# Block attention in a two-block layer kernel on one core: queries held backwards, the bias added by VectorE, 64-row products on alternate halves, the last softmax round ahead of its slabs, value slabs 512 columns wide

## The chip, the cores and the metric

One core of one Trainium2 chip runs the whole kernel. The metric is the device time of one execution in microseconds (us); lower is better. The profiled execution is one more execution, whose trace is read below.

## What is computed

Two transformer-like blocks on 256 tokens of width 1024. The change touches the first half of the first block, `hybrid_layer`, and there above all the block attention:

```
h = rmsnorm(x, norm_mix)
proj = h @ w_in                       # 27 slabs of 256 columns
qa, ka, va, ra, a_lr, qb, kb, vb, gates = split(proj)
oa = gla_chunked(qa, ka, va, log_a)   # 4 heads, chunks of 64 tokens, kv products k^T v
# block attention: 8 heads of 64, one block of 256 keys, so all keys are "own"
logit = qb @ kb^T * 64 ** -0.5 + bias_tab[:, t5_bucket(q_pos - k_pos)]
logit = where(k_pos <= q_pos, logit, -1e30)
ob = softmax(logit) @ vb
mixed = sigmoid(g_a) * (oa @ w_branch_gla) + sigmoid(g_b) * (ob @ w_branch_moba)
```

After it come w_out, two gated conv feed-forwards, a conformer block and a window attention of the second model. None of their code is changed.

## The kernel before, in words

All weights come from memory as slabs of 1 MB (128 partitions x 2048 floats) in a ring of three buffers (`raw`). A slab of the "mix" kind is split for precision: ScalarE copies it to `whi` (L785), VectorE and GpSimd subtract one half each into `wlo` (L1205, L743), and TensorE then makes three products for each 128x128 piece (`mm3`, L1776 to L1778: hi by hi, hi by lo, lo by hi). A slab of the "ada" kind is used unsplit, by TensorE's L1910. The order is written out by hand: every engine runs down the same list `LEAD` of 51 items, in which mix slabs g0 to g26 alternate with ada slabs until ada 23 stands between g21 and g22; g23 to g26 follow each other directly. An engine that waits in one item holds all that stands behind it in its own queue. ScalarE and VectorE split the slab three places ahead (`hi(Slab(n + RING))`, `lo(Slab(n + RING))`) at the start of each item.

Between the slabs, small pieces of the two attentions are hung on numbers g:

- g5 to g8 are the value slabs of the first attention and g13, g14 those of the block attention. `tokens` keeps the tokens still and streams 256 columns, 48 products a slab, into half a PSUM bank for each of the two token tiles; ScalarE copies each slab out (`drain`, L929). Items with a mix slab use banks 0 and 2 in turn, and a slab waits until the mix slab two before it was copied out (`mix_drained`).
- g10 and g11: the state products of the first attention (L2009), 64 rows of k each, first the four heads of chunk 0 (rows 0 to 63), then those of chunk 1 (rows 64 to 127), then at g11 chunk 2.
- g15, g18 and g21: the scores of the block attention in three rounds. Round 0 has queries 0 to 127 of 8 heads against 128 keys, rounds 1 and 2 have queries 128 to 255 of 4 heads each against 256 keys. For each head two f32 products go into the same place in PSUM banks 4 and 5: the 64-row product of query and key (L2064, even heads in rows 0 to 63 and bank 4, odd heads in rows 64 to 127 and bank 5), and a 128-row product of a reversing matrix `rev` with `brev`, the bias rows by distance, which adds the bias (L2066).
- `less_max` on VectorE: row maximum (L1445) and scores less maximum into `state` (L1449). ScalarE makes exponentials of it (L996). VectorE then sums, inverts and multiplies (L1528, L1530, L1532) and releases `p_done`. TensorE turns the result in eight transposes (L2048) into banks 6 and 7, and ScalarE copies these out (L1002). `less_max` of rounds 0, 1, 2 stands at g16, g19, g22, the normalising at g17, g20, g23, the transposes at g18, g21, g24, and the product with the values at g25 (L2078).

## Time and profile before

| | us |
|---|---|
| median of 3 runs | 1451.29 |
| the runs | 1450.57 to 1452.48 |
| the profiled execution | 1450.95 |
| its span, first to last instruction | 1449.2 |
| TensorE matmuls busy | 1398.1 (96%) |
| VectorE, ScalarE, GpSimd busy | 981.4, 824.7, 575.6 |
| mean granted TensorE clock | 0.991 of 2.4 GHz |

Busy time is time in which at least one instruction of the engine was under way. Consecutive matmuls overlap, so for their cost the distance of their starts counts, not the duration of one. The granted clock is either 1.00 or half; a mean between tells how much of the stretch was at half.

### The profile page before, as it was taken

How to read it: one execution, taken by the hardware profiler on the slowest of the kernel's cores; microseconds unless marked ns; L12 is line 12 of the kernel's file. 1: busy time of each engine (PE TensorE's matmuls, PEld its weight loads, DVE VectorE, ACT ScalarE, POOL GpSimd, SP SyncE). 2: the span in 40 equal slices, each digit the busy share in tenths (PEclk: the TensorE clock that was granted, in tenths of full speed). 3: DMA queues.
4: the chain of work that ended last, by engine and by line, in shares of the span. 5: the costliest groups of instructions: out<-in, count | busy, mean ns of one | idle time of the engine just before them, and what ended most of it. 6: DMA issues, size and time to landing. Idle time of an engine off the chain costs nothing.

```text
span 1449.2 us, 27974 instructions
## 1 busy us (share of the span) xinstructions
PE 1398.1 (96%) x11062; PEld 1310.0 (90%) x11062; DVE 981.4 (68%) x1302; ACT 824.7 (57%) x1179; POOL 575.6 (40%) x192
## 2 busy tenths in 40 slices
PE   5999999999999999999999999999999898999997
PEld 3899888999999999999999998999997757899997
DVE  3312554666889987859899977665665684765665
ACT  4632354555778856567888465545544474555543
POOL 2443334365422222453222233655654201465562
PEclk9999999999999999999999999999999999999999
DMA  7784565345344445674444455655545401544550
GB/s 283 270 313 185 222 234 204 146 176 187 123 172 171 173 175 200 252 275 162 170 166 169 162 204 219 233 203 208 224 177 223 186 30 59 198 181 175 188 187 30
DMA packets 39144, 272.09 MB, mean 188 GB/s; under 512 B 4436, under 2 KB 5588, under 8 KB 6414
## 3 DMA queue, kind: packets, MB, share of 16 engines
q1 hardware_dynamic: 39054, 270.81, 49.8%
q8 instruction: 66, 1.08, 0.3%
q14 instruction: 24, 0.20, 0.0%
HBM read 269.73 MB, written 1.06 MB: 187 GB/s over the span
## 4 chain that ended last, share of the span: by engine, by line
PE 86%; DVE 5%; ACT 4%; DMA 2%; POOL 1%; issue 1%; SPq 0%; DVEq 0%; ACTq 0%
PE ps L1776 22%; PE ps L1777 22%; PE ps L1778 22%; PE ps L616 9%; PE ps L1910 3%; ACT whi L785 2%; POOL wlo L743 1%; DMA raw<-w_dram 1%; PE ps L1813 1%; PE ps L2244 1%; DVE wlo L1205 1%; PE ps L2232 1%; DMA mv<-b_forget_dram 1%; PE ps L2066 1%; PE ps L2064 1%
## 5 line engine op out<-in xcount | busy, mean ns | idle before, releaser
L743 POOL TENSOR_TENSOR wlo<-raw,whi 128x1024 fp32r<-128x1024 f32 (+1 forms) x183 | 573.4, 3136 | 849.2 <-ACT whi L785 849.1
L785 ACT ACTIVATE whi<-raw 128x2048 fp32r<-128x2048 f32 x183 | 349.3, 1910 | 415.2 <-PE ps L1778 233.5
L1205 DVE TENSOR_TENSOR wlo<-raw,whi 128x1024 fp32r<-128x1024 f32 (+1 forms) x183 | 288.0, 1574 | 325.0 <-ACT whi L785 324.4
L1776 PE MATMUL ps<-h_hi,whi 128*128 128x256 f32 x1248 | 360.2, 289 | 4.8 <-POOL wlo L743 4.8
L1777 PE MATMUL ps<-h_lo,whi 128*128 128x256 f32 x1248 | 354.6, 284 | 0.0
L1778 PE MATMUL ps<-h_hi,wlo 128*128 128x256 f32 x1248 | 354.3, 284 | 0.0
L1776 PE MATMUL ps<-g_hi,whi 128*128 128x256 f32 x1040 | 298.4, 287 | 5.8 <-POOL wlo L743 2.6
L1777 PE MATMUL ps<-g_lo,whi 128*128 128x256 f32 x1040 | 294.9, 284 | 0.0
L1778 PE MATMUL ps<-g_hi,wlo 128*128 128x256 f32 x1040 | 294.8, 283 | 0.0
L1776 PEld LDWEIGHTS ps<-h_hi,whi 128*128 128x128 f32 x1248 | 240.9, 193 | 13.3 <-issue 12.8
L1777 PEld LDWEIGHTS ps<-h_lo,whi 128*128 128x128 f32 x1248 | 241.0, 193 | 0.5
L1778 PEld LDWEIGHTS ps<-h_hi,wlo 128*128 128x128 f32 x1248 | 240.9, 193 | 0.0
L1776 PEld LDWEIGHTS ps<-g_hi,whi 128*128 128x128 f32 x1040 | 200.1, 192 | 10.1 <-issue 6.9
L1777 PEld LDWEIGHTS ps<-g_lo,whi 128*128 128x128 f32 x1040 | 200.2, 192 | 0.3
L1778 PEld LDWEIGHTS ps<-g_hi,wlo 128*128 128x128 f32 x1040 | 200.2, 192 | 0.0
L616 PE MATMUL ps<-cvb,raw 128*128 128x256 f32 x704 | 155.3, 379 | 0.0
L616 PEld LDWEIGHTS ps<-cvb,raw 128*128 128x128 f32 x704 | 132.5, 190 | 17.3
L1776 PE MATMUL ps<-m_hi,whi 128*128 128x256 f32 x384 | 108.7, 283 | 0.0
L1777 PE MATMUL ps<-m_lo,whi 128*128 128x256 f32 x384 | 108.7, 283 | 0.0
L1778 PE MATMUL ps<-m_hi,wlo 128*128 128x256 f32 x384 | 108.7, 283 | 0.0
L533 DVE SCALAR_TENSOR_TENSOR cvb<-ps,cols,cvb 128x255 f32<-128x255 f32 (+1 forms) x176 | 76.5, 476 | 11.3 <-ACT cvb L455 6.7
L879 ACT ACTIVATE bufB<-gates,cols 128x256 f32 (+1 forms) x176 | 72.7, 499 | 17.9 <-DVE sra L1327 17.9
(270 smaller groups left out, 1958.7 us busy)
## 6 DMA issues: line engine op xcount, KB each, us to landing
raw<-w_dram SPq DMA_DIRECT2D x247, 1024.0 KB, 4.8
brev<-w_dram SPq DMA_DIRECT2D x2, 1024.0 KB, 6.8
gates<-w_dram SPq DMA_DIRECT2D x2, 1024.0 KB, 7.7
xlat<-xT_dram SPq DMA_DIRECT2D x1, 1024.0 KB, 4.9
brev<-bias_rows SPq DMA_DIRECT2D x1, 1024.0 KB, 8.9
brev<-ctxT_dram SPq DMA_DIRECT2D x1, 1024.0 KB, 10.2
sra<-w_dram SPq DMA_DIRECT2D x1, 1024.0 KB, 7.2
mqk<-w_dram SPq DMA_DIRECT2D x1, 1024.0 KB, 6.7
```

Source lines behind the costliest of these rows:

```text
L533: ins = dve.scalar_tensor_tensor(out, ps[:, 2 * par + half, m * T + src:m * T + src + n], w, out, ALU.mult, ALU.add)
L616: ins = pe.matmul(ps[:, 4 + m // 2, (m % 2) * T:(m % 2) * T + T], wf[:, k, m * P:m * P + P], cvb[:, par, k, :], start=(first and k == 0 an ...
L743: pool.tensor_tensor(wlo[:, g.slot, part], raw[:, g.slot, part], whi[:, g.slot, part].bitcast(F32), ALU.subtract).then_inc(lo2_done, 1)
L785: act.activation(whi[:, g.slot, :], raw[:, g.slot, :], ACT.Copy).then_inc(hi_done, 1)
L879: ins = act.activation(buf[:, t * T:t * T + T], vpad[:, t, bass.ds(k, T)], ACT.Copy, scale=w)
L1205: dve.tensor_tensor(wlo[:, g.slot, part], raw[:, g.slot, part], whi[:, g.slot, part].bitcast(F32), ALU.subtract)\
L1776: pe.matmul(out, w[0], x[0], start=start, stop=False, skip_group_check=True)
L1777: pe.matmul(out, w[0], x[1], start=False, stop=False, skip_group_check=True)
L1778: return pe.matmul(out, w[1], x[0], start=False, stop=stop, skip_group_check=True)
L1813: pe.matmul(ps[:, bank, m * T:m * T + T], w[i][:, k, m * P:m * P + P], x[0][:, k, :], start=(k == 0 and m == 0 and i == 0), stop=False, sk ...
L1910: ins = pe.matmul(ps[r:r + QUAD, bank, 0:SLABC], cnd[:, c:c + QUAD], w[:, t, :], start=(t < 4 and k == 0), stop=(t >= 4 and k == n - 1), s ...
L2064: pe.matmul(out, mqk[r0:r0 + DH, 0, h // 2, q0:q0 + P], mqk[r0:r0 + DH, 1, h // 2, 0:nk], start=(i % 512 == 0), stop=False, skip_group_che ...
```

## The change

Five edits, all in the stretch up to about 250 us.

1. The queries of the block attention are stored with each 128-token half reversed (`backwards`, a negative step in ScalarE's output). The scores then have the row order that the bias rows in `brev` already have, and `rev` and the products L2066 are gone. After the scores, VectorE adds `brev` to the scores in PSUM (a 128x1024 addition ahead of the row maximum in `less_max`); the wait for the bias rows moves from TensorE to VectorE. ScalarE's copy of the transposed probabilities writes backwards, so what follows is as it was.
2. The score products, now all of 64 rows, alternate between rows 0 to 63 and 64 to 127 from head to head. The state products at g10 do so too: for each head chunk 0, then chunk 1.
3. Round 2's `less_max` and normalising both move to the item ada 23 (from g22 and g23), ahead of VectorE's split of that item; its exponentials move there too on ScalarE. The transposes and their copy move from g24 to g23.
4. The value slabs hold 512 columns by half of the input width, two to a group. `tokens_wide` streams 512 columns, 24 products a slab, into banks 0 and 2. Both are copied out after the second slab of the pair (`drain_wide`), and the first slab of a pair waits for `mix_drained` once more before its second token tile.
5. The load of `xctx` into the buffer of `brev` waits for the last `less_max`, not for the last scores.

```diff
+        def backwards(a):
+            *outer, (step, n) = a.ap
+            return bass.AP(a.tensor, a.offset + step * (n - 1), [*outer, [-step, n]])
...
-                    sp.wait_ge(sc_done, 3)
+                    sp.wait_ge(sub_done, 3)
...
+            def drain_wide(out):
+                for s in range(2):
+                    act.activation(out[:, s, :], ps[:, 2 * s, :], ACT.Copy).then_inc(mix_drained, 1)
...
+                if (kind, g) == ("ada", N_ADA - 1):
+                    exponentials(2)
                 hi(Slab(n + RING))
...
+                    turned_back = backwards(flat(pt_of(r)).rearrange("p (a x) -> p a x", x=P))
+                    act.activation(turned_back, flat(ps[:, 6:8, :]).rearrange("p (a x) -> p a x", x=P), ACT.Copy).then_inc(pt_sb, 1)
...
+                dve.wait_ge(brev_in, 16)
                 dve.wait_ge(sc_done, r + 1)
+                order.mark(dve.tensor_tensor(by_parity, by_parity, bias, ALU.add))
+                dve.wait_ge(dve_order, order.value())
                 order.mark(dve.tensor_reduce(tiny[:, 32:32 + nb], sc, AX.X, ALU.max))
...
+            def tokens_wide(g, i, x, second):
+                w = weights(g, 4)
+                for s in range(2):
+                    if s and not i:
+                        pe.wait_ge(*second)
+                    for k in range(4):
+                        t = 4 * i + k
+                        ins = mm3(ps[:, 2 * s, :], [a[:, t, s * P:s * P + P] for a in x], [a[:, k, :] for a in w],
+                                  start=(t == 0), stop=(t == KT - 1))
+                ins.then_inc(slab_done, 1)
...
-                        tokens(Slab(AT[kind, g]), n % 4, H)
+                        tokens_wide(Slab(AT[kind, g]), 1 - g % 2, H, (mix_drained, g))
...
-                    for c in (0, 1) if g == 10 else (2,):
-                        s, r0 = c // 2, (c % 2) * CHUNK
-                        for h in range(H_GLA):
+                    for h in range(H_GLA):
+                        for c in (0, 1) if g == 10 else (2,):
+                            s, r0 = c // 2, (c % 2) * CHUNK
...
-                        pe.matmul(out, mqk[r0:r0 + DH, 0, h // 2, q0:q0 + P], mqk[r0:r0 + DH, 1, h // 2, 0:nk],
-                                  start=(i % 512 == 0), stop=False, skip_group_check=True)
-                        ins = pe.matmul(out, rev, brev[:, h, T - nk:T], start=False, stop=True, skip_group_check=True)
+                        ins = pe.matmul(out, mqk[r0:r0 + DH, 0, h // 2, q0:q0 + P], mqk[r0:r0 + DH, 1, h // 2, 0:nk],
+                                        start=(i % 512 == 0), stop=True, skip_group_check=True)
```

How the instructions stand on TensorE around round 1 of the scores (after slab g18), before; L2048 are the transposes of round 0, L1910 is the ada slab that follows:

```order
L2048 MATMUL ps<-consts,state 128x128 [waits probs_done]
L2048 MATMUL ps<-consts,state 128x128 x7
L2064 MATMUL ps<-mqk 128x256 [waits scores_less_max]
L2066 MATMUL ps<-brev,consts 128x256
L2064 MATMUL ps<-mqk 128x256
```

and after (the transposes are now L2089, the scores L2104, the ada slab L1951):

```order
L2089 MATMUL ps<-consts,state 128x128 [waits probs_done]
L2089 MATMUL ps<-consts,state 128x128 x7
L2104 MATMUL ps<-mqk 128x256 [waits scores_less_max]
L2104 MATMUL ps<-mqk 128x256 x3
L1951 MATMUL ps<-raw,cnd 32x256 [waits slab_landed1]
```

Where a score and a bias product alternated four times, four score products now stand together.

VectorE from the last `less_max` of round 1 to the end of round 2, before (L1205 is the split of a slab):

```order
L1445 TENSOR_REDUCE tiny<-ps 128x4 [waits scores_done]
L1449 TENSOR_TENSOR state<-ps,tiny 128x1024 [waits probsT_done,dve_order]
L1205 TENSOR_TENSOR wlo<-raw,whi 128x1024 [waits slab_hi_done]
L1528 TENSOR_REDUCE tiny<-state 128x4 [waits exp_done]
L1530 RECIPROCAL tiny<-tiny 128x4 [waits dve_order]
L1532 TENSOR_TENSOR state<-state,tiny 128x1024 [waits dve_order]
L1205 TENSOR_TENSOR wlo<-raw,whi 128x1024 [waits slab_hi_done] x2
L1445 TENSOR_REDUCE tiny<-ps 128x4 [waits scores_done]
L1449 TENSOR_TENSOR state<-ps,tiny 128x1024 [waits probsT_done,dve_order]
L1205 TENSOR_TENSOR wlo<-raw,whi 128x1024 [waits slab_hi_done]
```

and after, from the split of the slab ahead of round 2 (L1224 the split, L1468 the bias addition, L1482 to L1486 the normalising):

```order
L1224 TENSOR_TENSOR wlo<-raw,whi 128x1024 [waits slab_hi_done]
L1468 TENSOR_TENSOR ps<-ps,brev 128x1024 [waits scores_done,bias_landed]
L1470 TENSOR_REDUCE tiny<-ps 128x4 [waits dve_order]
L1474 TENSOR_TENSOR state<-ps,tiny 128x1024 [waits probsT_done,dve_order]
L1482 TENSOR_REDUCE tiny<-state 128x4 [waits exp_done]
L1484 RECIPROCAL tiny<-tiny 128x4 [waits dve_order]
L1486 TENSOR_TENSOR state<-state,tiny 128x1024 [waits dve_order]
L1224 TENSOR_TENSOR wlo<-raw,whi 128x1024 [waits slab_hi_done] x2
```

Round 2 goes one slab split earlier, in one piece, and each round begins with the addition.

ScalarE at the value slabs g5 to g8, before (L785 the split, L929 the copy out):

```order
L785 ACTIVATE whi<-raw 128x2048 [waits slab_used,slab_landed0]
L929 ACTIVATE gates<-ps 128x2x256 [waits slab_used]
L785 ACTIVATE whi<-raw 128x2048 [waits slab_used,slab_landed2]
L929 ACTIVATE gates<-ps 128x2x256 [waits slab_used]
L785 ACTIVATE whi<-raw 128x2048 [waits slab_used,slab_landed1]
L929 ACTIVATE gates<-ps 128x2x256 [waits slab_used]
```

and after (L790, L938):

```order
L790 ACTIVATE whi<-raw 128x2048 [waits slab_used,slab_landed0]
L790 ACTIVATE whi<-raw 128x2048 [waits slab_used,slab_landed2]
L938 ACTIVATE gates<-ps 128x512 [waits slab_used]
L938 ACTIVATE gates<-ps 128x512
L790 ACTIVATE whi<-raw 128x2048 [waits slab_used,slab_landed1]
```

The copies of a pair now stand together, behind the split that follows the pair's second slab in the list.

## Rows read from the trace of the kernel before

**Rows 1.** The page, busy time, share of the span, instructions, by engine.
```profile
PE 1398.1 (96%) x11062; PEld 1310.0 (90%) x11062; DVE 981.4 (68%) x1302; ACT 824.7 (57%) x1179; POOL 575.6 (40%) x192
```

**Rows 2.** Timeline, TensorE, round 0: start, duration, engine, line, operation, operands, count.
```profile
158.63 0.48 PE L2064 MATMUL ps<-mqk 64*128 64x128 f32 x2
...
165.30 1.07 PE L1910 MATMUL ps<-raw,cnd 128*32 128x256 f32 x16
```

**Rows 3.** Timeline, TensorE, round 1; then the 256-wide group of L2066, both rounds.
```profile
187.38 0.70 PE L2064 MATMUL ps<-mqk 64*128 64x256 f32 x2
...
192.40 1.07 PE L1910 MATMUL ps<-raw,cnd 128*32 128x256 f32 x16
...
L2066 PE MATMUL ps<-brev,consts 128*128 128x256 f32 x16 | 5.6, 431 | 0.0
```

**Rows 4.** Timeline, TensorE, the state products at g10 and at g11.
```profile
106.78 2.96 PE L2009 MATMUL ps<-gates,bufB 64*128 64x256 f32 x16
...
116.62 1.99 PE L2009 MATMUL ps<-gates,bufB 64*128 64x256 f32 x8
```

**Rows 5.** Timeline, TensorE, 64-row scores of the window attention, halves alternating.
```profile
1168.26 0.49 PE L2185 MATMUL ps<-m_hi,g_hi 64*128 64x512 f32 x2 [0.55 <-ACT tiny L1129]
1168.57 0.42 PE L2185 MATMUL ps<-m_lo,g_hi 64*128 64x512 f32 x2
1168.80 0.42 PE L2185 MATMUL ps<-m_hi,g_lo 64*128 64x512 f32 x2
```

**Rows 6.** Timeline, TensorE, 128-wide f32 products of one form.
```profile
125.38 0.60 PE L2022 MATMUL ps<-bufA,gates 128*128 128x128 f32 x4
```

**Rows 7.** Timeline, TensorE, value slab g7; then a group of two-pass f32 products.
```profile
77.23 0.28 PE L1777 MATMUL ps<-wlo,h_hi 128*128 128x256 f32 x1
77.35 0.28 PE L1778 MATMUL ps<-whi,h_lo 128*128 128x256 f32 x1
...
L616 PE MATMUL ps<-cvb,raw 128*128 128x256 f32 x96 | 21.2, 379 | 0.0
```

**Rows 8.** Timeline, ScalarE, while slab g6 is used.
```profile
75.07 1.91 ACT L785 ACTIVATE whi<-raw 128x2048 fp32r<-128x2048 f32 x1 [3.28 <-DMA raw<-w_dram]
76.88 0.58 ACT L929 ACTIVATE gates<-ps 128x512 f32<-128x512 f32 x1
```

**Rows 9.** Timeline, TensorE, round 2; window: length, busy by engine, clock, DMA.
```profile
241.36 1.89 PE L2048 MATMUL ps<-consts,state 128*128 128x128 f32 x8 [3.05 <-DVE state L1532]
242.90 0.56 PE L1776 MATMUL ps<-h_hi,whi 128*128 128x256 f32 x1
...
249.70 0.43 PE L2078 MATMUL ps<-state,mv 128*64 128x128 f32 x2
...
241.30:245.00 3.70, 3.64 (x18) 3.64 (x19) 3.31 (x2) 1.03 (x1) 2.22 (x1) 0.54 0.39 166
```

**Rows 10.** Timeline, TensorE, transposes of round 1.
```profile
213.01 0.28 PE L1778 MATMUL ps<-h_hi,wlo 128*128 128x256 f32 x1
213.31 1.09 PE L2048 MATMUL ps<-consts,state 128*128 128x128 f32 x8
```

**Rows 11.** Timeline, VectorE and ScalarE, round 1; the last is round 2.
```profile
206.86 1.21 DVE L1445 TENSOR_REDUCE tiny<-ps 128x4 f32<-128x1024 f32 x1
...
212.03 1.23 DVE L1532 TENSOR_TENSOR state<-state,tiny 128x1024 f32<-128x1024 f32 x1
...
209.36 1.06 ACT L996 ACTIVATE state<-state 128x1024 f32<-128x1024 f32 x1 [0.48 <-DVE state L1449]
...
226.46 3.71 ACT L785 ACTIVATE whi<-raw 128x2048 fp32r<-128x2048 f32 x2 [5.58 <-PE ps L1778]
```

**Rows 12.** One line's instructions, VectorE, PSUM and SBUF operands.
```profile
L1559 DVE TENSOR_TENSOR bufB<-ps,gates x2: 1210/1210/1211, 291.8 to 298.0; 128x1024 f32<-128x1024 f32 x2
```

**Rows 13.** Windows: length, busy PE PEld DVE ACT POOL, clock, DMA share, GB/s.
```profile
903.00:911.00 8.00, 6.16 (x41) 6.11 (x40) 7.28 (x6) 5.07 (x6) 7.62 (x3) 0.79 0.37 129
1202.00:1210.00 8.00, 6.54 (x57) 5.49 (x56) 3.89 (x12) 4.45 (x12) 0.00 (x0) 1.00 0.01 3
```

More of the change, by code:

```diff
@@ L324, in build @@
         wlr, alr = mv[0:RANK + 1, 0, :], mv[0:RANK + 1, 1, 0:T]
-        eye, rev, cum = (consts[:, i, :] for i in range(3))
+        eye, cum = (consts[:, i, :] for i in range(2))
         xctx = brev
@@ L1450, in less_max, with normalise @@
                    .then_inc(sub_done, 1)
+            def normalise(r):
+                nb = 8 if r == 0 else 4
+                pr = flat(state[:, 0, :, :]).rearrange("p (h k) -> p h k", h=nb)
+                dve.wait_ge(e_done, r + 1)
+                order.mark(dve.tensor_reduce(tiny[:, 40:40 + nb], pr, AX.X, ALU.add))
+                dve.wait_ge(dve_order, order.value())
+                order.mark(dve.reciprocal(tiny[:, 48:48 + nb], tiny[:, 40:40 + nb]))
+                dve.wait_ge(dve_order, order.value())
+                dve.tensor_tensor(pr, pr, tiny[:, 48:48 + nb, None].to_broadcast([P, nb, 1024 // nb]), ALU.mult)\
+                   .then_inc(p_done, 1)
             for n, (kind, g) in enumerate(LEAD):
[L1453 removed]
+                if (kind, g) == ("ada", N_ADA - 1):
                     less_max(2)
+                    normalise(2)
                 lo(Slab(n + RING))
@@ L2321 @@
                       (o_ra, V_W), (o_g, 2 * D)]:
+        if c0 in (o_va, o_vb):
+            for c in range(c0, c0 + width, 2 * SLABC):
+                for k in range(2):
+                    put("lead", AT["mix", i], win[k * D // 2:(k + 1) * D // 2, c:c + 2 * SLABC])
+                    i += 1
+            continue
         for c in range(c0, c0 + width, SLABC):
```

49 lines of the change are left out of this document (23 added, 26 removed).

## The prediction, made before the changed kernel ran

> **What bounds the kernel now.** I read the page first: TensorE is busy for 96% of the span, the next engine for 68% [rows 1]. So TensorE's own time counts nearly one for one, and work of the other engines counts only where TensorE waits for it. Then I went down TensorE's timeline at the places that the change touches, by distances of starts, since single durations overlap. Third I looked at the transposes, where TensorE meets the softmax: in round 2 it stands idle for 3.05 us until VectorE's multiplication ends, and the clock is at half for most of the 3.7 us behind that (mean 0.54, the 1.2 GHz level) [rows 9]. All the rest of the program is unchanged; I take its time as it is.
>
> **The change part by part**, against the profiled execution's span of 1449.2 us.
>
> *Score products.* Round 0 goes from 158.63 to 165.30: 6.67 us for 16 products, 0.417 each [rows 2]. Each f32 product is two records. Of one form, four 128-wide records stand in 0.60 us of which the last one's own length is about 0.28, so a record costs (0.60 - 0.28)/3 = 0.107 us [rows 6]; two would be 0.21. The other 0.2 us is what changing between 64 and 128 rows costs each time. Round 1 takes 192.40 - 187.38 = 5.02 us for 8 products, 0.627 each, and round 2 the same (x16 records of L2066 are two rounds) [rows 3]. Do products in different halves run at the same time? At g10 sixteen records, eight in each half one after the other, take 2.96 us; at g11 eight records of one half take 1.99. Two such groups in series would be nearly 4, so about 1.0 us already runs at the same time where the halves meet [rows 4]. And six 64x512 products in alternating halves start as three pairs, 0.31 and 0.23 apart, and are over 0.96 us after the first start [rows 5]; six in series at the 0.23 of one would need 1.4. So I count one half only. One 256-wide record more costs (1.99 - 0.70)/6 = 0.215 (eight records of one half less the first two [rows 3, 4]). Round 0: first product 0.417, six further records by 0.107, 1.06 us. Rounds 1 and 2: 0.627 + 2 x 0.215 = 1.06 each. Gain: 5.6 + 3.96 + 3.96 = **13.5 us**. If the halves did not overlap: round 0 0.417 + 14 x 0.107 = 1.9, the others 0.627 + 6 x 0.215 = 1.9, gain 11.0. If each change of half cost as a change of form does, half of the blocks goes: 8.4. I take 13.5, as rows 5 is the same pattern.
>
> *State products at g10.* Perfect alternation makes sixteen records as long as eight: 2.96 - 1.99 = **1.0 us** (between 0, if the queue already did what it can, and 1.0).
>
> *Value slabs.* Six slabs have 48 products of 256 columns, 0.12 us apart [rows 7]: 0.24 for two. A 512-wide one is not in the trace on full rows. From below: a two-pass f32 record, which also streams 512 column steps, costs 21.2/96 = 0.221 [rows 7]. From above: the last pair of half-array products came 0.23 after the one before [rows 5]. 144 products by 0.24 - 0.221 = 2.7 us, by 0.24 - 0.23 1.4. I take 0.221, the row on the full array: **2.6 us**. Off the path: ScalarE's copies, 1.16 where one 0.58 stood twice.
> TensorE: Matmul & The Clock Gate in the Trainium skill, section "Back-to-back issue gap", gives N/2.4 GHz plus about 2.5 ns, an estimate of 0.216 us for 512 columns; by it this term would be 3.5 us. The same rule makes 256 columns 0.109, where the trace has 0.12 [rows 7], so I don't take it; it is the page's form of the rival on cheaper products below.
>
> *The new wait behind a pair.* At g7 TensorE must have bank 0 back, which ScalarE now copies out only after g6. Before, the copy after g6 was at 76.88, held up by the split of a slab that landed at 75.07 (1.91 us), and ended at 77.46; g7's second product was at 77.23, so g7 began at about 77.0 [rows 7, 8]. That split is set by a landing, and the landing by an ada slab's end ahead of g6. g5 will be 0.44 us shorter, g6 too: the landing moves by the first, to 74.6, the copy ends at 77.0, and TensorE would be ready at 77.0 - 0.9 = 76.1. It waits **0.9 us** (0 to 1.1). Ahead of g9 and g15 stand the other products of g8 and g14, and they don't wait. Queued behind that wait are only TensorE's own slabs.
>
> *Round 2 ahead.* TensorE was idle for 3.05 us, counted from the last product's end; the next start could have been 0.28 - 0.12 = 0.16 ahead of that end (duration and distance in [rows 7]): 3.2 us. Behind that, at half clock, the transposes took 242.90 - 241.36 = 1.54 instead of about 1.0 (1.09 with the last one's tail in [rows 10]), and g25 249.70 - 242.90 = 6.80 instead of 48 x 0.12 + 0.2 = 5.9: 1.4 us. If the wait goes, so does the fall of the clock [rows 9]. What is late next? From the scores to the new place of the transposes TensorE has ada 23 (1.07 [rows 3]), g22 (5.9), two tiny products and g23 (5.9): 13 us. The chain needs the addition 1.22, maximum and difference 2.5, exponentials 1.1, sum to product 2.7 [rows 11, 12]: 7.6. It has 5 us to spare. What stands behind it: on ScalarE the split of g24, which waits for the end of g22 anyway (at 226.46) [rows 11], 6.9 us after the scores, and the exponentials end after 5. On VectorE its half of that split, due 8.9 us after the scores, when the chain has been through for 1.3 us; and g24 gets the transposes (1.0) as new cover. On SP the load of xctx goes out some 4 us later; behind it stand the loads of the first slabs after LEAD, which wait for the split of g24, later still. Gain: **4.6 us**.
>
> *The bias addition in rounds 0 and 1.* It costs 1.21 us as a PSUM and SBUF operation of the same size [rows 12], and with a short wait behind it 1.25. In round 0 ScalarE's exponentials wait for a slab's landing and split, several us after the difference is ready: hidden. In round 1 it is not: the transposes start at 213.31, just after VectorE's product ends (212.03 + 1.23), while the last slab product was at 213.01 and the next could have come at 213.13 [rows 10, 11]. The chain is already the later one by 0.18. The exponentials at 209.36 waited for the difference, so what is added there is added at its end. Against it, the slab whose landing starts the chain may come 0.3 us sooner, since the next load goes out later behind it. New wait 1.1 to 1.4 us, of which 0.18 was there: **-1.1 us**. Both ends of that lie below the idle time that was followed by half clock: 8.00 - 6.16 = 1.84 us idle and a mean clock of 0.79 in one stretch, 1.46 us idle and 1.00 in another [rows 13].
>
> *Writing backwards.* Five ScalarE copies of the same size; no row shows a negative step. At the old speed they cost nothing.
>
> **Sum:** 13.5 + 1.0 + 2.6 - 0.9 + 4.6 - 1.1 = 19.7 us. 1449.2 - 19.7 = 1429.5 of span; the profiled execution lies 1.75 over its span and the median 0.34 over that: 1431.6 us.
>
> **The rivals.**
> *Halves don't overlap for two-pass products, or not within one round.* For it: g10's overlap is only at the seam. Against: rows 5. Scores gain 11.0 and g10 nothing: 3.5 us less, 1435.1.
> *Round 1 becomes the new late chain and takes the clock along.* For it: 0.18 us of slack missing already, and the addition comes on top; if the landing is not sooner but 0.5 later, the wait is 1.9, and half clock for 3.4 us costs 1.5 more, as in round 2 [rows 9]: -2.2 us, 1433.8. Against: the idle of 1.46 that cost no clock [rows 13].
> *The wide slabs pay little:* 0.231 a product and both copies on the path: gain 1.4 - 1.1 instead of 1.7, 1433.0.
> *The wide products are still cheaper.* If column steps alone counted, 512 would cost what two of the 0.107 records of 256 steps cost [rows 6]: 0.214, a gain of 3.7 instead of 2.6, 1430.5. Against: the 0.221 of a 512-step record [rows 7].
> *Slower than before: ScalarE's reversed copies.* Place: the three copies of 1024 elements a partition, some 1.1 us each (0.58 for 512 [rows 8], 1.06 for exponentials of 1024 [rows 11]). The idle time behind them is of the order of the 5.58 us ahead of a split in rows 11. To eat up 19.7 us, each would have to take 5.5 + 19.7/3 = 12 us, eleven times as long. Nothing in the profile speaks for that; if it is twice as long it is hidden.
>
> **Chances.** My forecast 0.55; halves not overlapping 0.10; round 1 with clock 0.12; wide slabs poor 0.12; cheaper wide products or a fall of the clock fewer elsewhere 0.10; slower or no change 0.01. In the unchanged rest, waits like the 1.84 us one [rows 13] may keep or lose their fall of the clock, 1.5 us each. The range takes in these and the ends above: 1428.0 (cheap products, no wait at g7) to 1436.5 (halves in series and a poor round 1). A measurement can tell about 0.2%, 3 us, from no change; every case but the last is faster by more: faster 0.98, same 0.01, slower 0.01.
>
> **What would show it.** Right: no L2066; blocks of scores of 1.1 us; no wait of transposes in round 2, full clock there, and a wait of about 1.2 us in round 1; 0.9 us idle before g7; 512-wide products 0.22 apart. Wrong: blocks of 2 us (no overlap), half clock at round 1, a VectorE addition far over 1.2 us, ScalarE copies longer than 1.1 us that TensorE waits for.

## The result and the profile after

| | before | after |
|---|---|---|
| median | 1450.93 us (1450.04 to 1452.48, 4 runs) | 1431.95 us (1431.91 to 1432.49, 4 runs) |
| profiled execution | 1450.95 us, span 1449.2 | 1431.94 us, span 1430.2 |

The ratio is 0.9869, 95% interval 0.9855 to 0.9883: 19.0 us less, where the prediction said 19.7 (1431.6 us).

To see where the 19 us are, I cut each trace at two points of TensorE: the first product of slab g5 and the first product behind the attention (`ps<-mqk,ones`). The stretch between them holds the whole change.

| kernel | start of g5, us | stretch of the change, us | from there to the end, us |
|---|---|---|---|
| before | 63.13 | 207.81 | 1178.3 |
| after | 63.75 | 189.20 | 1177.3 |

18.6 us come from the stretch; the loads at the start took 0.6 more and the unchanged rest 1.0 less. In the fourteen traces of this case the start lies between 62.7 and 64.2 and the rest between 1176.2 and 1179.5, with no relation to what was changed. So the stretch, which is not touched by these, is what the comparisons below are made with, and a difference of under 2 us in medians says little.

The page after, TensorE's line (as rows 1):

```profile
PE 1379.1 (96%) x10886; PEld 1292.2 (90%) x10886; DVE 983.0 (69%) x1305; ACT 825.0 (58%) x1179; POOL 580.4 (41%) x192
```

TensorE's busy time fell by 19.0 us and its share stayed at 96%: it is still the bound.

**Score and state products.** Timeline of TensorE after, round 0, round 1 and g10 (start, duration, engine, line, operation, operands, count):

```profile
157.62 1.16 PE L2104 MATMUL ps<-mqk 64*128 64x128 f32 x16
158.71 0.42 PE L1951 MATMUL ps<-raw,cnd 128*32 128x256 f32 x4
...
180.76 1.13 PE L2104 MATMUL ps<-mqk 64*128 64x256 f32 x8
181.82 0.42 PE L1951 MATMUL ps<-raw,cnd 128*32 128x256 f32 x4
...
107.23 2.00 PE L2050 MATMUL ps<-gates,bufB 64*128 64x256 f32 x16
109.16 0.42 PE L1951 MATMUL ps<-raw,cnd 128*32 128x256 f32 x4
```

Against [rows 2] the block of round 0 is 158.71 - 157.62 = 1.09 us instead of 6.67, against [rows 3] rounds 1 and 2 are 1.06 instead of 5.02, and sixteen state records have the duration that eight had in [rows 4].

**Value slabs and the wait at g7.** Timeline of TensorE, then of ScalarE, after (as rows 7 and 8; L938 is `drain_wide`):

```profile
77.96 0.50 PE L1805 MATMUL ps<-whi,h_hi 128*128 128x512 f32 x1 [0.77 <-ACT gates L938]
78.30 0.40 PE L1806 MATMUL ps<-wlo,h_hi 128*128 128x512 f32 x1
78.53 0.40 PE L1807 MATMUL ps<-whi,h_lo 128*128 128x512 f32 x1
78.77 0.40 PE L1805 MATMUL ps<-whi,h_hi 128*128 128x512 f32 x1
...
75.52 1.91 ACT L790 ACTIVATE whi<-raw 128x2048 fp32r<-128x2048 f32 x1 [5.00 <-DMA raw<-w_dram]
77.33 1.07 ACT L938 ACTIVATE gates<-ps 128x512 f32<-128x512 f32 x2
```

The 512-wide products start 0.23 to 0.24 us apart. The six slabs together take 33.95 us instead of 35.46. Ahead of g7 TensorE waits 0.84 us (0.77 idle, the rest under the last product's tail).

**Round 1.** Timelines after of TensorE (L2089 are the transposes), VectorE, GpSimd and ScalarE (as rows 10 and 11; L1224 and L748 are VectorE's and GpSimd's half of the split of slab g22):

```profile
204.10 1.10 PE L2089 MATMUL ps<-consts,state 128*128 128x128 f32 x8 [1.38 <-DVE state L1486]
...
195.36 1.22 DVE L1468 TENSOR_TENSOR ps<-ps,brev 128x1024 f32<-128x1024 f32 x1
...
197.88 1.22 DVE L1474 TENSOR_TENSOR state<-ps,tiny 128x1024 f32<-128x1024 f32 x1
199.02 2.42 DVE L1224 TENSOR_TENSOR wlo<-raw,whi 128x1024 fp32r<-128x1024 f32 x1
201.36 1.21 DVE L1482 TENSOR_REDUCE tiny<-state 128x4 f32<-128x1024 f32 x1
...
197.95 2.40 POOL L748 TENSOR_TENSOR wlo<-raw,whi 128x1024 fp32r<-128x1024 f32 x1 [4.73 <-ACT whi L790]
...
195.96 1.91 ACT L790 ACTIVATE whi<-raw 128x2048 fp32r<-128x2048 f32 x1 [2.46 <-DMA raw<-w_dram]
```

The addition (L1468) takes 1.22 us. TensorE waits 1.54 us (1.38 idle and 0.16 under the tail), where it waited 0.18.

**Round 2** has no wait at all any more; the window has the clock at full speed, where rows 9 has 0.54 (window: length, busy PE PEld DVE ACT POOL, clock, DMA share, GB/s):

```profile
219.23 1.04 PE L2089 MATMUL ps<-consts,state 128*128 128x128 f32 x8
220.02 0.36 PE L1805 MATMUL ps<-h_hi,whi 128*128 128x256 f32 x1
...
218.00:222.00 4.00, 4.00 (x36) 4.00 (x35) 2.55 (x4) 3.43 (x5) 4.00 (x2) 1.00 0.49 162
```

**Writing backwards.** ScalarE's copy of the probabilities, by line after, the first of three (the others took 1018 and 1020 ns):

```profile
L1021 ACT ACTIVATE state<-ps x1: 1022/1022/1022, 185.0 to 185.0; 128x1024 f32<-128x1024 f32 x1
```

It took 1.02 us before too; the queries' copies take 0.578, like straight ones.

### The profile page after: what moved, and what is told of

Its sections match the earlier page's. It is cut to its first block, busy times and chain, and to the rows that moved or that the text cites. A ratio compares the mean times of both kernels' runs of the same rounds, so it can differ in the third digit from the quotient of the medians.

```text
span 1430.2 us, 27629 instructions
## 1 busy us (share of the span) xinstructions
PE 1379.1 (96%) x10886; PEld 1292.2 (90%) x10886; DVE 983.0 (69%) x1305; ACT 825.0 (58%) x1179; POOL 580.4 (41%) x192
## 3 DMA queue, kind: packets, MB, share of 16 engines
HBM read 269.66 MB, written 1.06 MB: 189 GB/s over the span
## 4 chain that ended last, share of the span: by engine, by line
PE 83%; ACT 5%; DVE 5%; DMA 3%; POOL 2%; issue 1%; DVEq 0%; SPq 0%; ACTq 0%
PE ps L1805 22%; PE ps L1806 21%; PE ps L1807 21%; PE ps L621 9%; DMA raw<-w_dram 3%; PE ps L1951 2%; ACT whi L790 2%; POOL wlo L748 2%; PE ps L1842 1%; PE ps L2283 1%; DVE wlo L1224 1%; PE ps L2271 1%; ACT bufA L1146 1%; PE ps L2224 1%; ACT mqk L871 1%
## 5 line engine op out<-in xcount | busy, mean ns | idle before, releaser
L748 POOL TENSOR_TENSOR wlo<-raw,whi 128x1024 fp32r<-128x1024 f32 (+1 forms) x183 | 578.2, 3163 | 825.4 <-ACT whi L790 825.2
L790 ACT ACTIVATE whi<-raw 128x2048 fp32r<-128x2048 f32 x183 | 349.5, 1911 | 413.3 <-PE ps L1807 226.0
L1224 DVE TENSOR_TENSOR wlo<-raw,whi 128x1024 fp32r<-128x1024 f32 (+1 forms) x183 | 280.7, 1535 | 308.1 <-ACT whi L790 306.5
L538 DVE SCALAR_TENSOR_TENSOR cva<-ps,cols,cva 128x255 f32<-128x255 f32 (+1 forms) x176 | 76.6, 477 | 9.0 <-ACT cva L460 4.3
```

The costliest lines, as they stand in the source:

```text
L538: ins = dve.scalar_tensor_tensor(out, ps[:, 2 * par + half, m * T + src:m * T + src + n], w, out, ALU.mult, ALU.add)
L748: pool.tensor_tensor(wlo[:, g.slot, part], raw[:, g.slot, part], whi[:, g.slot, part].bitcast(F32), ALU.subtract).then_inc(lo2_done, 1)
L790: act.activation(whi[:, g.slot, :], raw[:, g.slot, :], ACT.Copy).then_inc(hi_done, 1)
L1224: dve.tensor_tensor(wlo[:, g.slot, part], raw[:, g.slot, part], whi[:, g.slot, part].bitcast(F32), ALU.subtract)\
```

## The experiments

All ratios are to the kernel before, measured beside it. "Stretch" is the time from g5 to the end of the attention as above, 189.20 us in the changed kernel's first trace.

### 1. Were the form changes or the removed products the gain?

The kernel before, with the bias products behind all score products of a round:

```diff
                    for h in range(8) if r == 0 else range(4 * r - 4, 4 * r):
                        i = place(h, r) * nk
                        out = ps[:, 4 + i // 512, i % 512:i % 512 + nk]
...
                        pe.matmul(out, mqk[...], mqk[...], start=(i % 512 == 0), stop=False, skip_group_check=True)
+                   for h in range(8) if r == 0 else range(4 * r - 4, 4 * r):
+                       i = place(h, r) * nk
+                       out = ps[:, 4 + i // 512, i % 512:i % 512 + nk]
                        ins = pe.matmul(out, rev, brev[:, h, T - nk:T], start=False, stop=True, skip_group_check=True)
```

> The kernel before, with one edit: in each round the bias products stand behind all score products, not one behind each. The same products are made, so no work is saved; the form changes between 64 and 128 rows once a round instead of at each product, and score products of the two halves stand next to each other. Theory (the 0.2 us belongs to each change of form, and halves overlap): round 0 is 1.06 for the scores, 0.2 for the change, 16 records at 0.107, 3.0 us instead of 6.67; rounds 1 and 2 1.06 + 0.2 + 8 records at 0.215 = 3.0 instead of 5.02. Together 7.7 us less than before, of which round 2's part counts only if its softmax isn't late by as much: its transposes wait for a chain that starts with these scores, so that part, 2.0, may show as shorter idle time or not at all. 1443 to 1445. Rival (score products are dear in themselves, whatever stands between them): 5 to 6 us per round, the same time as before, 1451, and then the gain of the change came from the products that were left out.

Measured: 1441.97 us (1441.42 to 1442.26), ratio 0.9938 (0.9924 to 0.9951); stretch 200.22, 7.6 less than before. Timeline of TensorE in round 0:

```profile
159.37 1.16 PE L2064 MATMUL ps<-mqk 64*128 64x128 f32 x16
160.46 2.05 PE L2069 MATMUL ps<-brev,consts 128*128 128x128 f32 x16
```

The scores take 1.09 us, the bias products 1.98; rounds 1 and 2 take 2.98 instead of 5.02. That is 7.7 us less in the three blocks, as expected. The median is 9.0 less and lies under the 1443 to 1445 of the expectation; beside the stretch, the start took 0.7 more and the rest, which the edit doesn't touch, 2.0 less. So 7.6 of the 13.5 us were paid for switching between 64 and 128 rows and for the missing overlap, and could be had by reordering one loop, without VectorE's addition. The other 5.8 are the removed products themselves. How the 7.6 divide between the switching and the missing overlap, this run doesn't separate.

### 2. How far does the overlap of the halves reach?

The changed kernel with even heads, then odd heads, and g10 chunk by chunk:

```diff
-                    for h in range(H_GLA):
-                        for c in (0, 1) if g == 10 else (2,):
+                    for c in (0, 1) if g == 10 else (2,):
+                        for h in range(H_GLA):
...
-                    for h in range(8) if r == 0 else range(4 * r - 4, 4 * r):
+                    for h in sorted(range(8) if r == 0 else range(4 * r - 4, 4 * r), key=lambda h: h % 2):
```

> The changed kernel with the halves in groups: all even heads of a round, then all odd ones, and the state products at g10 chunk by chunk as before. Theory (products in different halves run side by side only where two groups meet): g10 0.97 longer as before. Score blocks: in series they would be 1.9 us each against 1.07 now, so at most 0.85 more each, 2.5 in all; with an overlap at the seam as at g10 of before (1.0 of 4.0), 0.5 us of each block is saved again, so about 0.4 each, 1.1 in all. Together UP by 1.0 + 1.1 to 2.5: 1434.0 to 1435.4. Rival (the score products were cheap because the form no longer changes, and alternation gives nothing): blocks stay 1.07, and only g10 moves.

Measured: 1432.78 us (1432.24 to 1435.39), ratio 0.988 (0.9865 to 0.9895). Timeline of TensorE in round 0, at g10 and in round 1:

```profile
157.92 1.71 PE L2104 MATMUL ps<-mqk 64*128 64x128 f32 x16
...
106.57 2.96 PE L2050 MATMUL ps<-gates,bufB 64*128 64x256 f32 x16
...
181.60 1.14 PE L2104 MATMUL ps<-mqk 64*128 64x256 f32 x8
```

Round 0 is 0.55 us longer, g10 0.96, rounds 1 and 2 not at all, where the theory had about 0.4 each. The time is under the 1434.0 forecast for a second reason: the stretch, 189.76, is only 0.56 longer than in the first trace of the changed kernel: the wait of round 1 was 0.64 and not 1.54 (experiment 5). In rounds 1 and 2 a group is four records, and the eight start as four pairs, 0.013 us apart within a pair. In round 0 and at g10, with groups of eight, the first four start alone, and only from the fifth on do two start within 0.006 us. So TensorE takes up a record of the other half up to four records early. The rows don't name a record's half; but the first record of each half is a long one at g10 (0.48 us, the others 0.376), and the second such record stands at the sixth place in time, where the program has it at the ninth. The next run tests it; in it the halves alternate in groups of four records (two heads):

> The changed kernel with the halves alternating in groups of four records (two heads of one half, then two of the other) instead of groups of one product: round 0 and the state products at g10. With groups of eight records round 0 took 1.64 us and g10 2.89, with alternating products 1.09 and 1.93; with groups of four in rounds 1 and 2, 1.07 as when alternating. Theory (TensorE's queue runs ahead by some four records of the other half): groups of four are as good as alternating ones, 1.09 and 1.93, time as the changed kernel's. Rival (only the direct neighbour of the other half runs alongside, and rounds 1 and 2 were spared for another reason): round 0 some 1.3 to 1.5, g10 2.4.

Measured: 1431.68 us (1429.78 to 1432.88), ratio 0.9869 (0.9852 to 0.9885). Timeline of TensorE in round 0 and at g10:

```profile
156.62 1.26 PE L2104 MATMUL ps<-mqk 64*128 64x128 f32 x16
...
106.14 2.10 PE L2050 MATMUL ps<-gates,bufB 64*128 64x256 f32 x16
```

Both are 0.10 longer than alternating, far below the rival's 0.2 to 0.5. The theory holds, with a record (0.107 in [rows 6], here 0.10) lost at a seam; its stretch is 188.95. Strict alternation, which the change chose, is the best of the three; in rounds 1 and 2 either order would have done. The Trainium skill (TensorE: Matmul & The Clock Gate, section "The mechanism") says that matmuls start in program order and are not reordered. Two starts together from the fifth record on, where eight of one half stand ahead of the other's first, speak against that for two halves of the array, and here the trace decides.

### 3. What do the wide slabs bring?

```diff
-                        tokens_wide(Slab(AT[kind, g]), 1 - g % 2, H, (mix_drained, g))
+                        tokens(Slab(AT[kind, g]), n % 4, H)
```

with the copies and the layout of the slabs as before.

> The changed kernel with value slabs 256 wide again. In the traces of before and after a value slab takes 5.94 and 5.70 us, and the wait at g7 that the pair's copies bring is 0.84 us. Theory (512-wide products start 0.230 apart, not 0.221): slabs give back 1.5 us, the wait gives 0.8, so the time goes UP by 0.6 to 0.7, to about 1432.6. My prediction's own terms (2.6 and 0.9) would make it 1433.7. Rival (the wait at g7 isn't due to the pair's copies but to the landing ahead of them): idle time stays at g7, and the time goes up by the whole 1.5, to 1433.5.

Measured: 1431.8 us (1430.57 to 1434.54), ratio 0.9876 (0.9859 to 0.9892). From g5 to the scores of round 0 the trace has 94.54 us instead of 93.87: 0.67 more, as the theory said, and no wait at g7. But the stretch as a whole is 189.04, 0.16 less, since at round 1 the transposes waited 0.71 us (0.55 idle and the tail) and not 1.54. Timelines of TensorE, VectorE, GpSimd and ScalarE there:

```profile
204.33 1.09 PE L2087 MATMUL ps<-consts,state 128*128 128x128 f32 x8 [0.55 <-DVE state L1484]
...
197.97 1.23 DVE L1468 TENSOR_REDUCE tiny<-ps 128x4 f32<-128x1024 f32 x1
199.23 1.23 DVE L1472 TENSOR_TENSOR state<-ps,tiny 128x1024 f32<-128x1024 f32 x1
200.37 1.22 DVE L1222 TENSOR_TENSOR wlo<-raw,whi 128x1024 fp32r<-128x1024 f32 x1
...
197.67 2.39 POOL L748 TENSOR_TENSOR wlo<-raw,whi 128x1024 fp32r<-128x1024 f32 x1 [3.09 <-ACT whi L790]
...
195.68 1.91 ACT L790 ACTIVATE whi<-raw 128x2048 fp32r<-128x2048 f32 x1 [0.83 <-DMA raw<-w_dram]
```

The split of slab g22 began 1.1 us ahead of ada 22 here and 0.25 us behind its start in the changed kernel, as its load took 4.70 us from issue to landing and not 6.04. That is experiment 5.

### 4. The two new waits, mended

Copy the pair out ahead of ScalarE's split:

```diff
+                if (kind, g) == ("mix", 6):
+                    act.wait_ge(slab_done, n + 1)
+                    drain_wide(va[:, :, 0:2 * SLABC])
                 hi(Slab(n + RING))
```

> The changed kernel; after g6 ScalarE copies the value pair out ahead of the split of the next slab instead of behind it. Theory (g7 waits for these copies, which stand behind a split that starts with a landing at 75.5): the copies start at the end of g6 and end before 77.0, the wait of 0.84 at g7 goes, and nothing else is late: DOWN by 0.8, to 1431.1. Rival: the split that comes 2.1 us later is itself waited for at the next slab: same time, 1431.9, with idle time ahead of g8 in place of g7.

Measured: 1430.95 us (1430.06 to 1433.29), ratio 0.9865 (0.9848 to 0.9881); stretch 191.47, 2.3 more than in the first trace of the changed kernel, which is round 1's wait and the clock behind it (experiment 5). The wait at g7 is gone, and the same 0.9 us stand at g9, which needs a bank of the pair g7 and g8. TensorE and ScalarE:

```profile
93.68 0.39 PE L1808 MATMUL ps<-h_hi,whi 128*128 128x256 f32 x1 [0.82 <-ACT gates L938]
...
75.89 1.08 ACT L938 ACTIVATE gates<-ps 128x512 f32<-128x512 f32 x2 [5.66 <-PE ps L1810]
...
91.23 1.91 ACT L790 ACTIVATE whi<-raw 128x2048 fp32r<-128x2048 f32 x1 [5.85 <-DMA raw<-w_dram]
```

The copies behind g8 stand behind a split that starts at 91.23; in the changed kernel it started at 90.38, and the copies were through in time. From g5 to g9 it is 30.33 us against 30.26: nothing gained. The rival was right, one slab further on than it said. What moved the split is the load that it waits for. Counted from the start of g5 it was issued 0.8 us sooner (20.2 instead of 21.0), but it took 7.60 us instead of 5.52 and landed later. In all three kernels of this experiment that wait at g9 this load took 7.35 to 7.60, in the other eleven traces 5.16 to 6.61. Why it is longer when issued sooner stays open; that the mend can't pay is shown only for loads like these.

Round 1's transposes behind ada 23:

```diff
+                    if g == N_ADA - 1:
+                        turn_probs(1)
...
-                if g in (18, 21, 23):
+                if g in (18, 23):
```

> The changed kernel; round 1's transposes stand behind round 2's scores and ada 23, some 2.1 us of TensorE work further on. Theory (TensorE waits there 1.54 us for VectorE's normalisation and does nothing else): the wait goes, the transposes' own 1.0 us stays: DOWN by 1.5, to 1430.4. Rival (what follows them is next: the copy of the transposes and the products of round 1 are then late, or round 2's scores overwrite something that waits for them): the wait moves to the next place, 1431.5 to 1432.5.

Measured: 1431.34 us (1429.79 to 1431.63), ratio 0.9867 (0.9851 to 0.9883); stretch 187.55, 1.65 less. TensorE:

```profile
202.96 1.13 PE L2108 MATMUL ps<-mqk 64*128 64x256 f32 x8
204.02 1.07 PE L1951 MATMUL ps<-raw,cnd 128*32 128x256 f32 x16
205.02 1.09 PE L1990 MATMUL ps<-consts,state 128*128 128x128 f32 x8
```

No idle time, although the load took 6.03 us as in the changed kernel's trace. The wait didn't move on; the theory was right. Both mends together:

> The changed kernel with both mends: the value pair's copies ahead of ScalarE's split at g6, and round 1's transposes behind ada 23. If the two waits are separate: 0.84 + 1.54 less, 1429.6. If either mend only moves its wait: 1430.4 to 1431.2. Rival: the offset moves a wait late in the program to the other side of a fall of the clock, as happened between before and after at 1099 to 1118 us: 1.2 us more or less than the sum.

Measured: 1430.55 us (1429.43 to 1432.0), ratio 0.9863 (0.9848 to 0.9878); stretch 188.01. The load took 6.72 us and the transposes waited 0.06; g9 waited 0.67, and behind round 2's transposes the first product came 0.5 us later than in the other traces of that order (18.83 us for g23 to g25 instead of 18.30), for a reason that the trace doesn't name. As the two runs before it say, one mend works and the other moves its wait to g9.

The last version keeps the transposes' new place and makes the first pair narrow again:

> The changed kernel with round 1's transposes behind ada 23, and with the first pair of value slabs 256 wide again, the other two pairs wide. The first pair wide saves 0.5 us and brings a wait of 0.84 behind it. Theory: no wait ahead of g7; g7 and g8 wide meet none, as g9 has other products ahead of it: 0.3 less than with the transposes moved alone, which was 1431.3 (and 1.46 less than the changed kernel on the path up to there): 1430 to 1431. Rival (the second wide pair meets at g9 the wait that the first one met at g7, as when the pair's copies went ahead of the split): 0.5 us more than with the transposes moved alone, 1431.8.

Measured: 1429.84 us (1429.5 to 1430.31), ratio 0.986 (0.9843 to 0.9876), the lowest median of all. Its stretch is 189.17, though, 1.6 more than with the transposes moved alone. g9 waits 0.64 us, and from g5 to g9 it is 0.3 more; 0.3 more stand at g14 and behind it; and the load of this run took 7.63 us, so that even behind ada 23 the transposes wait 0.97. So the narrow pair is no gain by the traces, and the rival was right on the place of the wait; by medians it isn't slower. The three kernels with the transposes moved have twelve runs, median 1430.2 us, 1429.4 to 1432.0; the changed kernel has eight (below), median 1432.2, 1429.7 to 1433.9. That the mend of the transposes is worth its wait of 1.5 us is shown in the trace; the medians, 2.0 apart, agree with it and wouldn't show it alone.

### 5. What sets the wait of round 1?

The changed kernel without the addition of the bias in round 1 (heads 0 to 3, not 4 to 7 as the expectation has it, get no bias there, so this part of the computation is missing):

```diff
+                if r != 1:
                     order.mark(dve.tensor_tensor(by_parity, by_parity, bias, ALU.add))
```

> The changed kernel without the bias addition in round 1, which leaves the bias of heads 4 to 7's first four out of what is computed. TensorE waits 1.54 us at round 1's transposes now. Theory of the prediction (the addition is added at the chain's end): 1.22 us shorter, so the wait falls to 0.3 and the time by 1.2, to 1430.7. Theory 2 (VectorE's split of g22 took 2.42 instead of 1.41 us because GpSimd's half of it had begun first, which the addition's delay brought about): VectorE's split comes ahead of GpSimd's again, takes 1.2 to 1.4, the chain is 2.2 shorter, the wait is gone, and the time falls by 1.5, to 1430.4. Rival (the wait is set by the landing of the slab, not by VectorE): no change.

Measured: 1431.51 us (1429.98 to 1432.4), ratio 0.9867 (0.9852 to 0.9882); stretch 187.89, 1.3 less. The wait is 0.28. But its load took only 4.79 us; the fair comparison is with the traces of short loads (4.70 to 5.21, the table below), whose wait is 0.7. So at such a load the addition itself costs 0.4, not 1.2. VectorE and GpSimd show why:

```profile
197.46 2.38 DVE L1224 TENSOR_TENSOR wlo<-raw,whi 128x1024 fp32r<-128x1024 f32 x1
...
196.35 2.41 POOL L748 TENSOR_TENSOR wlo<-raw,whi 128x1024 fp32r<-128x1024 f32 x1 [3.42 <-ACT whi L790]
```

VectorE's split of the slab, without the addition, began 1.1 us into GpSimd's half of the same split and ended 1.08 us after GpSimd (198.76, 199.84). With the addition and a short load it began after GpSimd was through (200.37, GpSimd's end 200.06) and took its own 1.22. Theory 2 named the right pair of instructions and had the sign wrong: the split is short when it comes late.

The changed kernel once more, for a second trace:

> The changed kernel itself once more, for a second trace. In its first trace the transposes of round 1 waited 1.54 us, and the load of the slab whose split starts that chain took 6.04 us from issue to landing; in the traces of four variants that don't touch this place it took 4.70 to 7.22 and the wait was 0.6 (4.70, 5.12, 5.21) to 2.1 (7.22). Theory (the load's length of this run sets the wait, not the kernel): a landing within 5.3 us goes with a wait of 0.6, one of 6.0 with 1.5. Rival (the wait is the changed kernel's own): 1.54 again, whatever the load takes. Time 1430.5 to 1432.5 either way, and 1177 to 1178.5 us from the first product behind round 2's output block to the end, as in all traces so far (1176.5 to 1178.5).

Measured: 1433.47 us (1429.73 to 1433.91), ratio 0.9877 (0.986 to 0.9894), over the 1430.5 to 1432.5 expected; stretch 191.59, 2.4 more than in the first trace of the same kernel. TensorE, VectorE, GpSimd, ScalarE, and a window behind the wait:

```profile
204.84 1.89 PE L2089 MATMUL ps<-consts,state 128*128 128x128 f32 x8 [2.11 <-DVE state L1486]
206.67 1.96 PE L2104 MATMUL ps<-mqk 64*128 64x256 f32 x8
...
199.20 2.99 DVE L1224 TENSOR_TENSOR wlo<-raw,whi 128x1024 fp32r<-128x1024 f32 x1
...
198.71 2.40 POOL L748 TENSOR_TENSOR wlo<-raw,whi 128x1024 fp32r<-128x1024 f32 x1 [5.30 <-ACT whi L790]
...
196.71 1.91 ACT L790 ACTIVATE whi<-raw 128x2048 fp32r<-128x2048 f32 x1 [3.04 <-DMA raw<-w_dram]
...
205.00:208.75 3.75, 3.75 (x20) 2.68 (x23) 3.08 (x1) 1.66 (x3) 2.00 (x1) 0.55 0.38 157
```

The load took 6.77 us, the wait was 2.27, and the clock fell to half behind it (0.55, the 1.2 GHz level): 0.7 for the longer wait, 0.8 for the transposes and 0.8 for the scores of round 2. The load (from its issue on SyncE to its landing, which starts ScalarE's split), the wait and the clock, in all traces that have the changed order and the addition at this place:

| load of g22's slab, us | wait at round 1's transposes, us | clock behind it |
|---|---|---|
| 4.70, 5.12, 5.15, 5.21 | 0.71, 0.64, 0.65, 0.71 | full |
| 5.69 | 1.19 | full |
| 6.04 (first trace) | 1.54 | full |
| 6.77 (second trace) | 2.27 | half |
| 7.22 | 2.14 | half |

That is the theory: the wait belongs to the load's length in that run. From 5.7 on the wait is the load's length less 4.5 us, and up to 5.2 it stays at 0.7, where VectorE's chain with the addition is the later one. (At 7.22 VectorE's split came first again and took 1.23, which is why it waits a little less.)

The traces without the addition at this place lie on the same line, down to 0.18: the kernel before had a load of 4.69 us, issued at the same distance, 5.81 us ahead of the ada slab, and a wait of 0.18; the grouped kernel of experiment 1 had 4.81 and 0.31; the one of this experiment 4.79 and 0.28. So what the addition does is to keep the wait from falling below 0.7. It costs 0.4 to 0.5 us at the shortest loads and, by this line, nothing from 5.2 on; the last is an estimate, as no trace has a long load without the addition. And the short wait of the kernel before was luck that one trace couldn't show: with a load of 6.04 the same line gives it 1.54.

### 6. Round 2 back at its old place

```diff
-                if g in (18, 21, 23):
+                if g in (18, 21, 24):
```

and likewise for the maximum, the exponentials and the normalising; the addition stays on VectorE.

> The changed kernel with round 2's softmax and transposes back at their old places (g22 to g24), the bias addition staying on VectorE. Theory of the prediction: the wait of the transposes is back (3.2 us and the addition's 1.25 on the same chain, 4.4), and half clock for some 3.4 us behind it (1.4): UP by about 5.9, 1437.8, with the granted clock near 0.5 in the 3.5 us behind the wait. Rival 1: the addition is absorbed, as the slab chain ahead of it comes sooner: up by 4.6, 1436.5. Rival 2: the fall of the clock belongs to the place in the program, not to the wait: it would be there in the changed kernel too, which it isn't; then up by 3.2 to 4.4 only, with no half clock.

Measured: 1436.33 us (1433.65 to 1437.41), ratio 0.9906 (0.989 to 0.9923). By medians 4.4 us more than the changed kernel's first four runs, but the trace of the fastest run shows a stretch of 190.97, only 1.8 more. A second trace was wanted:

> The kernel with round 2 back at its old place once more. Its first profiled run was its fastest, 1433.65 us beside 1436.2 to 1437.4 of the others: there TensorE was idle for 2.51 us ahead of round 2's transposes and the clock stayed full behind it. Theory (an idle stretch of that length is near the edge, and the other runs lost the clock there): a run of 1436 to 1437 shows half clock behind the wait, 1.4 us more, or a wait that is longer by 1 or 2 us. Rival (the other runs lost their 2.7 us elsewhere): the same 2.5 us idle, full clock, and the time is in the tail.

Measured: 1436.01 us (1433.64 to 1436.89), ratio 0.9901 (0.9884 to 0.9917); stretch 190.99. The rows of the first trace, TensorE, VectorE, GpSimd and the window behind the wait:

```profile
226.04 1.09 PE L2086 MATMUL ps<-consts,state 128*128 128x128 f32 x8 [2.51 <-DVE state L1484]
...
218.43 2.14 DVE L1222 TENSOR_TENSOR wlo<-raw,whi 128x1024 fp32r<-128x1024 f32 x1
221.45 1.23 DVE L1222 TENSOR_TENSOR wlo<-raw,whi 128x1024 fp32r<-128x1024 f32 x1 [0.71 <-ACT whi L790]
224.05 1.94 DVE L1484 TENSOR_TENSOR state<-state,tiny 128x1024 f32<-128x1024 f32 x1
...
213.68 5.82 POOL L748 TENSOR_TENSOR wlo<-raw,whi 128x1024 fp32r<-128x1024 f32 x2 [7.49 <-ACT whi L790]
...
226.10:229.80 3.70, 3.70 (x32) 3.70 (x33) 1.23 (x1) 3.12 (x3) 1.91 (x1) 1.00 1.00 421
```

Two steps of my expectation fell. The addition was absorbed: VectorE's split again ended 1.08 us after GpSimd's (219.49, 220.57; the POOL row holds two halves, of 3.45 and 2.41 us), whenever it began, and with the addition ahead of it it only stood there for less time, 2.14 us instead of 3.41. The next split came ahead of GpSimd's and took 1.23 instead of 3.27, and the last product of the softmax then stood behind GpSimd's, 1.94 instead of 1.23. Altogether TensorE waited less than in the kernel before, 2.67 us (2.51 idle and 0.16 under the tail) against 3.21. And this wait, the same in both traces, took no clock along, while 2.27 and 2.14 us at round 1 did. In the traces the move of round 2 is worth 2.7 us of wait (18.30 us for g23 to g25 and the transposes, 213.40 to 231.71, against 21.03, 211.79 to 232.82), with nothing for the clock. Over all eight runs undoing it cost more, 4.1 us in the median (1436.3 against 1432.2). The second trace, of a run 1.9 us longer than the first, has these 1.9 outside the stretch, 1.1 at the start and 0.7 in the rest. The 1.4 us between 2.7 and 4.1 no trace shows; they stay open.

## Why the prediction was right, and where it wasn't

The sum was 19.7 and the stretch gave 18.6. The mechanisms were right for the products, the wait at g7 and round 2; the size was wrong for the value slabs, and the mechanism for round 1. Term by term:

- **Score products**, predicted 13.5: 5.58 + 3.96 + 3.96 = 13.5. The record costs of [rows 3, 4, 6] and the overlap of [rows 5] carried over exactly, 1.06 predicted for each block, 1.06 to 1.09 measured. Experiment 1 shows the two halves of the term apart.
- **State products**, predicted 1.0: 0.96. Groups of eight gave it back.
- **Value slabs**, predicted 2.6 (its own multiplication, 144 x 0.019, gives 2.7): 1.5. This is the term that was mis-sized. The step was to take 0.221 for a 512-wide product, from a two-pass product, over the 0.23 of the last pair in [rows 5]; the second was the right row. With its start-up a slab's product costs 33.95/144 = 0.236 us, where the 256-wide one costs 35.46/288 = 0.123, and 144 times the difference, 0.246 less 0.236 before rounding, is the 1.5. The lower end of the range (1.4) held. The estimate after the Trainium skill's formula (TensorE: Matmul & The Clock Gate, section "Back-to-back issue gap"), 0.216, was farther off than either.
- **Wait at g7**, predicted 0.9 (0 to 1.1): 0.84, by the mechanism given, though the size is partly luck. Counted from the start of g5, TensorE was ready 0.51 us sooner than before, not 0.9, as the slabs are shorter by less; and ScalarE's split began 0.17 sooner, not 0.44. The two misses cancel. Experiment 4 adds that the wait goes when the pair's copies stand ahead of the split, or the first pair is narrow, but then stood at g9 in all three traces.
- **Round 2 ahead**, predicted 4.6: 23.14 - 18.30 = 4.8 against the kernel before. As a difference of two kernels this is right; as the worth of the edit alone it is less sure, since undoing it cost 2.7 in the trace. Of the other 2.1, 0.5 is the shorter wait of the undone kernel (2.67 against 3.21) and 1.6 is half clock, which the kernel before had behind 3.05 us of idle time and the undone one hadn't behind 2.51.
- **Bias addition in round 1**, predicted -1.1: -1.36 in the first trace, and right there for the wrong reason. The step "the exponentials waited for the difference, so what is added there is added at its end" left out that VectorE's split behind it was waiting for GpSimd, which absorbs the addition except at the shortest loads (0.4 left at 4.79 us). What made the wait longer is the load, 6.04 us against 4.69, which I had held to come sooner if anything: by the line of experiment 5 the load alone accounts for 1.35 of the 1.36.
- **The rival of round 1 with the clock** (1433.8) is no rival but one of the kernel's own cases: the second trace is it, 1433.91 us, with a wait of 2.27 and half clock behind it. By its first four runs (1431.91 to 1432.49) the kernel looked steadier than by all eight (1429.73 to 1433.91).
- **Reversed copies**, predicted 0: 0.

13.5 + 0.96 + 1.5 - 0.84 + 4.84 - 1.36 = 18.6, the whole stretch. Nothing else in it moved. That the forecast median, 1431.6, lies 0.35 us beside the measured one is in part luck: the sum is 1.1 over the stretch, start and rest together gave 0.3 back, a fourth run lowered the median before by 0.4, and the kernel's own runs are up to 4.2 us apart.

## What to carry to other kernels

Price a product by the distance of starts in the row that streams as many columns through the same path, and put products of different row counts into blocks: each change between 64 and 128 rows cost 0.2 us here, twice what a 128-wide record costs. Where an engine waits for another that shares a resource with it (here VectorE's splits behind GpSimd's), work put ahead of that wait is nearly free as long as it fits into it, and work taken away ahead of it brings nearly nothing. A place where TensorE meets a chain that starts with a load should have a microsecond or two of other TensorE work in front of it: one trace shows one length of that load, and it varied from 4.7 to 7.6 us.

## What the runs showed of the chip that I had not expected

- TensorE starts a record for the other half of the array up to four records ahead of its place: two groups of four overlap wholly (1.07 us in rounds 1 and 2, as when alternating), groups of eight by half (2.89 instead of 1.93), groups of four in a block of sixteen all but a record (2.03).
- A VectorE operation with two SBUF operands that begins while GpSimd's is under way ends 1.08 or 1.09 us after GpSimd's, in all 74 places between 150 and 260 us of the fourteen traces where VectorE's half of a split began behind GpSimd's, from starts 0.1 to 2.7 us into it; if VectorE begins first it takes 1.23 and GpSimd's 3.4 to 3.5 instead of 2.40. Operations that read PSUM aren't touched: with narrow slabs the maximum and the difference began 0.3 and 1.6 us into GpSimd's half (197.97 and 199.23) and took 1.23 each. The Trainium skill (SBUF — State Buffer, section "SBUF: two separate sides") calls this an exclusive lock of a shared port pair, held for a whole instruction; these rows agree with it.
- The length of an idle stretch alone doesn't tell whether the clock falls: 1.98 and 2.11 us idle at round 1 were followed by 0.57 and 0.55, and 2.51 and 2.50 at round 2 by 1.00. The kernel before and the grouped one had nearly the same idle time at round 2, 3.05 and 3.04 us, and the mean clock of the 3.7 us behind was 0.54 in the one and 0.71 in the other, where it fell later (0.83 in the next 3.7). What else decides is open. The grouped kernel's rows:

```profile
234.56 1.09 PE L2048 MATMUL ps<-consts,state 128*128 128x128 f32 x8 [3.04 <-DVE state L1532]
...
234.40:238.10 3.70, 3.54 (x22) 3.54 (x23) 3.42 (x2) 1.02 (x1) 2.33 (x1) 0.71 0.48 199
```
